# Moving operands of a Strassen FFN on another residue mod 256, with its matmuls in another order

## The reference

```python
def _swiglu(u, w_in, w_out):
    h = u @ w_in
    a, b = h[..., :D_FF], h[..., D_FF:]
    return (jax.nn.silu(a) * b) @ w_out
...
    x = x + 0.5 * _swiglu(_rmsnorm(x, norm_ffn1[i]), ffn1_w_in[i], ffn1_w_out[i])
    ...
    x = x + 0.5 * _swiglu(_rmsnorm(x, norm_ffn2[i]), ffn2_w_in[i], ffn2_w_out[i])
```

## Time and profile before

| | us |
|---|---|
| median of 3 runs | 1880.62 |
| lowest and highest | 1880.25, 1882.64 |
| profiled execution, its own time | 1879.91 |
| its span | 1878.1 |
| TensorE busy, 13850 matmuls | 1855.2 |
| weight loads busy, 13850 loads | 1834.6 |
| VectorE, ScalarE, GpSimd busy | 1251.5, 866.9, 329.5 |
| granted clock of TensorE, mean | 0.996 of 2.4 GHz |

### The profile page before, as it was taken

One profiled execution on the slowest core, in us unless ns is written; L12 is line 12 of the kernel. 1 busy time (PEld: TensorE's weight loads), 2 busy tenths in 40 slices (PEclk: granted clock), 3 DMA queues, 4 the chain that ended last, 5 costly groups with the idle time before them and its releaser, 6 DMA issues.

```text
span 1878.1 us, 34441 instructions
## 1 busy us (share of the span) xinstructions
PE 1855.2 (99%) x13850; PEld 1834.6 (98%) x13850; DVE 1251.5 (67%) x1999; ACT 866.9 (46%) x1518; POOL 329.5 (18%) x352
## 2 busy tenths in 40 slices
PE   8999999999999999999999999999999999999998
PEld 8999999998999999999999999999989999999998
DVE  7874487668884488679853886563546888548853
ACT  7552355347552355346532553232334665235532
POOL 2220122131220122132201221300010322012112
PEclk9999999999999999999999999999999999999999
DMA  8773576334763576347644763231113576357632
GB/s 207 166 149 105 128 167 148 108 85 95 166 147 108 127 167 150 107 107 165 146 131 102 171 141 101 86 102 68 57 45 103 117 169 152 108 120 167 135 93 82
DMA packets 116830, 234.71 MB, mean 125 GB/s; under 512 B 13184, under 2 KB 15248, under 8 KB 116672
## 3 DMA queue, kind: packets, MB, share of 16 engines
q1 hardware_dynamic: 77440, 160.59, 28.7%
q0 software_dynamic: 38208, 69.42, 22.5%
q10 hardware_dynamic: 1024, 2.49, 0.4%
HBM read 228.92 MB, written 3.53 MB: 124 GB/s over the span
## 4 chain that ended last, share of the span: by engine, by line
PE 93%; DVE 4%; ACT 2%; DMA 1%; issue 1%; DVEq 0%; ACTq 0%
PE ps L1850 49%; PE ps L1840 39%; DVE w_lo L1231 1%; PE ps L1895 1%; PE ps L2167 1%; PE ps L2233 0%; DVE u L1285 0%; DMA raw_z<-in_ffn_in 0%; PE ps L2170 0%; DMA x<-in_x 0%; PE ps L2032 0%; PE ps L2157 0%; DVE rstd L1302 0%; ACT w_hi L726 0%; PE ps L2142 0%
## 5 line engine op out<-in xcount | busy, mean ns | idle before, releaser
L1850 PE MATMUL ps<-u,w_hi 128*128 128x288 f32 x4928 | 984.0, 295 | 11.7 <-DVE w_lo L1231 4.5
L1850 PEld LDWEIGHTS ps<-u,w_hi 128*128 128x128 f32 x4928 | 790.6, 188 | 16.4 <-DVE w_lo L1231 9.4
L1850 PE MATMUL ps<-u,w_lo 128*128 128x288 f32 x2464 | 727.1, 295 | 0.0
L1850 PEld LDWEIGHTS ps<-u,w_lo 128*128 128x128 f32 x2464 | 462.6, 188 | 0.0
L1840 PE MATMUL ps<-h_hi,w_hi 128*128 128x288 f32 x1386 | 294.4, 293 | 0.0
L1840 PE MATMUL ps<-h_lo,w_hi 128*128 128x288 f32 x1386 | 294.3, 293 | 0.0
L1840 PE MATMUL ps<-h_hi,w_lo 128*128 128x288 f32 x1386 | 294.3, 293 | 0.0
L726 ACT ACTIVATE w_hi<-w_raw 128x768 fp32r<-128x768 f32 (+3 forms) x164 | 136.0, 836 | 316.6 <-PE ps L1840 240.2
L1231 DVE TENSOR_TENSOR w_lo<-w_raw,w_hi 128x768 fp32r<-128x768 f32 (+3 forms) x164 | 168.8, 1038 | 160.6 <-ACT w_hi L726 158.4
L1840 PEld LDWEIGHTS ps<-h_hi,w_lo 128*128 128x128 f32 x1386 | 220.4, 188 | 0.0
L1840 PEld LDWEIGHTS ps<-h_hi,w_hi 128*128 128x128 f32 x1386 | 220.3, 188 | 0.0
(11 more groups left out here) (268 smaller groups left out, 2123.5 us busy)
## 6 DMA issues: line engine op xcount, KB each, us to landing
raw_a<-in_ffn_in SPq DMA_DIRECT2D x132, 256.0 KB, 4.2
w_raw<-in_ffn_out SPq DMA_DIRECT2D x64, 384.0 KB, 3.2
raw_y<-in_ffn_in SPq DMA_DIRECT2D x88, 256.0 KB, 3.6
raw_x<-in_ffn_in SPq DMA_DIRECT2D x88, 256.0 KB, 2.7
raw_x<-in_ffn_in POOLq DMA_DIRECT2D x88, 256.0 KB, 6.5
raw_y<-in_ffn_in POOLq DMA_DIRECT2D x88, 256.0 KB, 4.9
raw_z<-in_ffn_in POOLq DMA_DIRECT2D x88, 256.0 KB, 5.1
w_raw<-in_ffn_out SPq DMA_DIRECT2D x64, 320.0 KB, 3.0
```

The lines of the kernel that those rows point to most:

```text
L1850: mm = pe.matmul(dst, w, m, start=prod in ("M1", "M2", "M5") and kp == 0 and p == 0, stop=kp == KP - 1 and p == 2, skip_group_check=prod i ...
```

## The change

Two things. `u7` is placed at residue 128, so its high parts have the residue of the weights and its low parts residue 0; what lies behind keeps its residues (addresses are 256 lower). And a product that is not in an opening group is issued by a new function: eight matmuls with high parts (for each K group, high weights and low weights), then four with low parts.

```diff
-    align(256)
+    align(256, 128)
     u_at = region(KP * 7 * 2 * HALF * 4)
     u7 = sb("u7", [P, KP, 7, 2, HALF], F32R, at=u_at)
     align(256, 128)
...
+            def product_whole(f, ph, prod, n):
+
+                u = f.unit(ph, prod, n)
+                dst = r_bank(n) if prod in ("M5", "M3") else q_bank(f, ph, n) if prod == "M2" else p_bank(n)
+                piece = PIECES.index(MOVING[prod])
+                for part in range(2):
+                    for kp in range(KP):
+                        w = slice(PLACE[u] + kp * P, PLACE[u] + (kp + 1) * P)
+                        for ring in (w_hi, w_lo) if part == 0 else (w_hi,):
+                            mm = pe.matmul(dst, ring[:, w], u7[:, kp, piece, part, :],
+                                           start=prod in ("M1", "M2", "M5") and kp == 0 and part == 0 and ring is w_hi,
+                                           stop=kp == KP - 1 and part == 1,
+                                           skip_group_check=prod in ("M3", "M4", "M6", "M7"))
+                mm.then_inc(unit_used, 1)
+
...
                     for prod, n in products:
                         product_waits(f, ph, prod, n)
                     part = needs[products[0][0]]
+                    if len(products) == 1 and (ph or part in seen):
+                        product_whole(f, ph, *products[0])
+                        continue
                     for kp in range(KP):
```

## The result

The changed kernel takes 1891.28 us (median of 5 runs, 1888.80 to 1893.63) against 1881.93 us (5 runs, 1880.25 to 1883.27) for the kernel before: a ratio of 1.0049, interval 1.0037 to 1.0061. It is 9.3 us slower. The forecast was 1878.9 with a range to 1890; rival 2 had named 1889.2.

What follows compares the result with a forecast made beforehand. TensorE bounds the kernel: number of matmuls times step. New-order products -1.5 us and the 24 old-order products -0.2 sum to -1.7 us, other terms 0, giving 1878.9 us (counted as no difference), range 1871 to 1890.

Steps and rivals of the forecast that it cites:

- rival 2: Output projections behind the product phases drop to the slower step, 1.76 us per stretch, 1889.2 us if all six; chance 0.26.
- What bounds the kernel: TensorE: time is number of matmuls times step; product waits only 11.4 us, none inside a long stretch of products.
- 592 products: FFN products taking the new order and residue: 1582.5 ns each, 2.6 less than before, -1.5 us (bounds -6.3 to +8.6).
- Output projections: Code and residues unchanged; six stretches at 130.0 ns and two at 133.3 as before, 0 us (bounds -3.5 to +10.3).
- the slower case: Whole kernel slower by more than 0.2% (3.8 us); chance 0.26.
- rival 3: All matmuls: residues have no effect, the step levels come from chance alignments; 1880.6 us, chance 0.05.
- waits: TensorE at the product lines: waits stay near 11 us as before, 0 us change.
- later low parts: First K group's low parts in a product are read seven steps (0.9 us) later; no wait arises.
- the moved inputs of the mLSTM: Normalised mixer inputs swap residues but still alternate; taken as 0, though leaving the slower step would win 5.1 us.
- the granted clock: TensorE clock: 1.00 of 2.4 GHz in every stretch read, and it cannot rise.

Runs made afterwards that it cites:

- m1_streams: New kernel without the computation: only streams of 128x288 matmuls, other engines idle; steps 133.3 ns at residue 0, 131.7 at 128, halves of h 133.3 or 130.0.
- e3_tail_old: The changed kernel with the last product of each product phase back in the old order; 1891.41 us, ratio 1.0061 to the kernel before.
- m2_memory: Matmul streams alone, first put at 130.0 ns, then products, then halves of h: 130.0 behind old-order products at residue 0, 133.3 behind twelve matmuls in new order.
- e1_residue: The kernel before with only the residue of `u7` changed, order as before; 1888.90 us, ratio 1.0052.
- e2_order: The kernel before with only the new order of products, `u7` still at residue 0; 1893.43 us, ratio 1.0069.
- e4_tail_new: The kernel before with only the last product of each product phase in the new order; 1887.13 us, ratio 1.0035.
- e8_before_kick: The kernel before with one matmul of 64 columns added ahead of the second output tile in each output phase; 1886.84 us, ratio 1.0035.

## Why the prediction was wrong

- **What bounds the kernel**: right. The number of matmuls times the step is the time. One reading was wrong: a wait does lie inside a phase of products, at 329 us, and behind it the stream had another level.
- **592 products**: wrong in sign, small in size. The constants were right (133.3 and 131.8 in the last tile, 133.3 and 131.7 in m1_streams), but a change of residue was taken at the alternation's price: -5.1 ns for the pair. Measured, a product in the new order takes 12 x 132.49 = 1590 ns, so the pair costs 2.3 more than the constants' 1587.6. -1.5 us were forecast; against 1585.1 ns before, 1590 make 592 x 4.8 = +2.8 us, and with waits 1.4 us shorter (10.0 for 11.4) the phases of products grew by 1.1 us.
- **Output projections**: this is the step that failed. I wrote that the cadence is chosen by what runs ahead, and then took "six fast and two slow stretches, as now: 0 us". Its bound, +10.3, was the outcome (+10.2): what was put at nothing was the whole loss. The argument against rival 2 ("six of eight now choose the fast one right behind a matmul at residue 0") looked at the last matmul only. e3_tail_old and m2_memory show that matmuls further back count, and the trace before held the hint: the products ahead of both slow output phases ran at 131.2, those ahead of the six phases at 130.0 ran at 132.2. A level that hands itself on through 924 matmuls is a state, and a change to those matmuls puts it at risk.
- **Rival 2**: right in its outcome, by luck in its reason. It blamed the run of four matmuls at residue 0 at the end of a product; e1_residue has no such run, e3_tail_old none ahead of the outputs, and both have all outputs at 133.3. Its sum also says that it outweighs the gain of 1.7 us "from three on"; one stretch of 1.76 us does.
- **Chances**: once seen as a state that only one pattern hands on, the slower case deserves most of the chance, not 0.26. The range ended at 1890 because it added +10.3 to a gain of 1.7 us that was not there.
- **The rule that was weighed**: rival 3 (residues are nothing) is refuted by the streams alone: 133.3 at residue 0 and 131.7 at 128, nothing else running. The Trainium skill, "TensorE: Matmul & The Clock Gate", "Step-by-step: what each phase is for", gives the moving operand and the weights independent read ports. It says nothing of where they lie; the conclusion that their place has no influence was mine, and these steps do not agree with it.
- **Other terms**: waits were 1.4 us less where 0 was forecast; later low parts and the moved inputs of the mLSTM show no cost. The 1.6 us less in the mixer are the granted clock, which the prediction read at 1.00 in its stretches alone: the same fall stands in the profiled executions of e2_order, e3_tail_old and e4_tail_new, and is missing in those of e1_residue and e8_before_kick, so neither residue nor order decides it.

What stays open is the mechanism in the chip: what differs in it when the step is 133.3 and when it is 130.0. The runs show states, what hands them on and what sets them, not their place. Open is also what gives the stream its state behind the waits at the beginning of an FFN.

## What to carry to other kernels

When matmuls follow each other without a wait, read the step (length over count) of each long stretch, not the busy share. Where the same code shows two steps, it is in two states: find out which stretch hands it to which, and set the state on purpose before orders or addresses are compared, or a difference of half a per cent says little about the edit. Here an address layout that alternates by itself lost 0.4% alone and won 0.5% with five short extra sequences, while the planned reordering lost 0.5%, in output matmuls that it did not touch.

## What the runs showed of the chip that I had not expected

- A stream of 288-column matmuls has steps of 130.0, 131.1, 131.7, 132.2, 132.5, 132.8 or 133.3 ns in these patterns at one clock, constant for hundreds of matmuls, the same with all other engines idle as beside DMA at 160 GB/s.
- The alternation of residues 0 and 128 has two levels, 130.0 and 133.3, below and at those of the constants (131.7 and 133.3). One matmul of 64 columns moved every fast stream to the slow level, and a slow one to the fast level in some states, not in all.
- Four matmuls at residue 0, 24 others and one of 32, 64 or 128 columns end in 130.0 from eight beginnings of eight. Without the four, the same small matmul is right in four of eight.
- How a stream comes out of a wait differs between executions: the same instructions gave products at 132.2 ns in one and 130.9 in another (before and e8_before_kick, first window), and one kernel ran from 1875.8 to 1898.7 us.
